# A gap of 64 bytes in front of the arena: it begins at a multiple of 128 bytes of a partition

## The reference

```python
for l in range(DEPTH):
    h = rms_norm(x, attn_norm[l])
    proj = h @ w_in[l]
    ...
    merged = g[:, :, 0] * o_a + g[:, :, 1] * o_b + g[:, :, 2] * o_c
    x = x + merged @ w_out[l]
    h2 = rms_norm(x, mlp_norm[l])
    x = x + jnp.square(jax.nn.relu(h2 @ w_up[l])) @ w_down[l]
```

## Time and profile before

| | |
|---|---|
| median of 3 runs | 2616.77 us (2615.76 to 2617.32) |
| profiled execution | 2626.14 us |
| span in it, first to last instruction | 2624.4 us |
| mean granted TensorE clock, share of full speed | 0.963 |
| TensorE busy with matmuls | 2446.8 us, 93% of the span |
| VectorE busy | 1946.6 us, 74% |
| ScalarE busy | 1388.1 us, 53% |
| read from main memory | 458.85 MB, 175 GB/s over the span |

### The profile page before, as it was taken

How to read it: one execution, slowest core, us unless ns; L and a number is a source line. 1 busy time by engine, 2 the same in 40 slices (tenths; PEclk the granted TensorE clock), 3 DMA queues, 4 the chain that set the end, 5 groups by cost and what they waited for, 6 DMA issues and landing times. The chain is left out here.

```text
span 2624.4 us, 46404 instructions
## 1 busy us (share of the span) xinstructions
PE 2446.8 (93%) x18912; PEld 2318.6 (88%) x18912; DVE 1946.6 (74%) x3284; ACT 1388.1 (53%) x2545; POOL 12.9 (0%) x20
## 2 busy tenths in 40 slices
PE   7899999988999999889998979999988999998998
PEld 6699999977999999879998879997788999976998
DVE  5477788754877886788887778886458889856884
ACT  6444555355455543646644556746463674434663
POOL 0000000000000000000000000000000000000000
PEclk8799999988999999989999999999989999988999
DMA  5124567721155678304565624573334457632552
GB/s 219 48 97 147 213 244 288 303 107 65 65 193 193 228 290 304 125 35 147 191 257 224 241 89 159 195 298 113 144 129 147 159 194 289 258 114 77 193 181 93
DMA packets 64084, 462.89 MB, mean 176 GB/s; under 512 B 7232, under 2 KB 7424, under 8 KB 8064
## 3 DMA queue, kind: packets, MB, share of 16 engines
q1 hardware_dynamic: 63872, 459.92, 47.5%
HBM read 458.85 MB, written 1.05 MB: 175 GB/s over the span
## 5 line engine op out<-in xcount | busy, mean ns | idle before, releaser
L770 PE MATMUL psum<-arena_rounded,upper_rounded 128*128 128x256 f32 (+2 forms) x5112 | 1450.9, 284 | 94.7 <-PEq L659 27.9
L771 PE MATMUL psum<-arena_rounded,upper_rounded 128*128 128x256 f32 (+2 forms) x5112 | 1437.4, 281 | 0.0
L772 PE MATMUL psum<-arena_rounded,ring_rounded 128*128 128x256 f32 (+2 forms) x5112 | 1436.8, 281 | 0.0
L770 PEld LDWEIGHTS psum<-arena_rounded,upper_rounded 128*128 128x128 f32 (+2 forms) x5112 | 972.1, 190 | 114.5 <-issue 62.7
L569 DVE TENSOR_TENSOR ring_rounded<-ring,upper_rounded 128x1024 fp32r<-128x1024 f32 (+4 forms) x958 | 840.0, 897 | 311.0 <-ACT upper_rounded L560 306.1
L560 ACT ACTIVATE upper_rounded<-ring 128x1024 fp32r<-128x1024 f32 (+4 forms) x958 | 751.6, 795 | 567.9 <-PE psum L772 483.5
L771 PEld LDWEIGHTS psum<-arena_rounded,upper_rounded 128*128 128x128 f32 (+2 forms) x5112 | 973.8, 190 | 0.7 <-issue 0.5
L772 PEld LDWEIGHTS psum<-arena_rounded,ring_rounded 128*128 128x128 f32 (+2 forms) x5112 | 972.3, 190 | 0.1
L591 DVE SCALAR_TENSOR_TENSOR ada_sum<-ring,small,ada_sum 128x1024 f32<-128x1024 f32 x168 | 214.9, 1279 | 1.3
L2369 DVE SCALAR_TENSOR_TENSOR arena<-psum,cols,arena 128x255 f32<-128x255 f32 (+1 forms) x352 | 153.3, 478 | 64.6 <-ACT arena L2336 61.5
L2336 ACT ACTIVATE arena<-psum,cols 128x256 f32<-128x256 f32 x176 | 89.5, 561 | 76.1 <-PE psum L772 76.0
(11 more groups left out here) (499 smaller groups left out, 2453.3 us busy)
## 6 DMA issues: line engine op xcount, KB each, us to landing
ring<-stream_dram SPq DMA_DIRECT2D x434, 1024.0 KB, 4.9
const<-const_dram SPq DMA_DIRECT2D x1, 1540.0 KB, 14.2
x<-x_dram SPq DMA_DIRECT2D x1, 1024.0 KB, 4.9
out_dram<-x SPq DMA_DIRECT2D x4, 256.0 KB, 2.1
cols<-cols_dram SPq DMA_DIRECT2D x1, 978.0 KB, 11.0
const<-const_dram SPq DMA_DIRECT2D x1, 67.0 KB, 4.6
pos<-positions_dram SPq DMA_DIRECT2D x1, 64.0 KB, 5.4
cols<-cols_dram SPq DMA_DIRECT2D x1, 4.0 KB, 4.4
```

What stands on the lines that cost most here:

```text
L770: pe.matmul(out, upper, x[0][:, b.k, :], start=(b.k == 0), stop=False)
L771: pe.matmul(out, upper, x[1][:, b.k, :], start=False, stop=False)
L772: ins = pe.matmul(out, lower, x[0][:, b.k, :], start=False, stop=(b.k == nk - 1))
```

## The change

`Chip.__init__` gets a small function that allocates a tensor that nobody uses, as large as is needed to bring the next start to `rest` modulo `edge`. It is called once, ahead of the arena, with 128: the arena and its rounded views move from byte 112,448 to 112,512. All other tensors stay where they are, and the instructions are the same.

```diff
         self.rounded_tensors = {}
 
+        def begin_at_multiple_of(edge, rest=0):
+
+            gap = (rest - (nc.sbuf_base + 31) // 32 * 32) % edge // 4
+            if gap:
+                sb(f"gap_{nc.sbuf_base}", gap)
+
         def sb_rounded_too(name, n, cuts=()):
 
             t = sb(name, n)
...
         self.small = sb("small", 176)
         self.stat = sb("stat", 8 * T)
         self.cos, self.pos = sb("cos", T), sb("pos", T, I32)
+        begin_at_multiple_of(128)
         self.arena = sb_rounded_too("arena", ARENA, ARENA_CUTS)
```

## The result

The changed kernel takes 2666.76 us (median of 4 runs, 2665.74 to 2667.93) against 2616.32 us of the kernel before on the same chip: a ratio of 1.0193, 95% interval 1.0175 to 1.0210. It is 50 us slower, and above the range that was forecast. The profiled execution took 2665.7 us.

What follows compares the result with a forecast made beforehand. The prediction took the spacing of TensorE's back-to-back float32r matmuls in project to bound the kernel. All terms summed to 0 against the median of 2616.8 us, giving 2617 us, range 2578 to 2640 us.

Steps and rivals of the forecast that it cites:

- What bounds the kernel: TensorE in project's three matmul lines: time is a count times a spacing, with 6.6 or 11.2 ns excess per matmul.
- One third at 113.3 ns and two thirds at 117.9 ns: Mix of spacings of L771's matmuls before the change, put at 116.3 ns on average.
- the long kind: Stretches before the change with 312 matmuls of L771 in 110 us, 117.9 ns apart; the short kind has 113.3 ns.
- The terms put at 0: Added instructions, waits, semaphores and transfers, VectorE and ScalarE work, and plain fp32 matmuls: each forecast to change nothing.
- the mix stays: Float32r matmuls keep their present shares of both spacings, 0 us; 2612 to 2622 us, chance 0.40.
- the address as such does not decide between the kinds: Float32r matmuls: both spacings occur at the same address modulo 128, so the choice looks settled when TensorE starts again.
- The upper bound: Float32r matmuls: if all took the long spacing, 5,000 x 4.5 ns = 23 us more.
- a spacing longer than any of today: Float32r matmuls: outside the range, unpriced; a still longer spacing shares the chance 0.27 with the long kind spreading.
- The slower one: Rival: the long spacing spreads at restarts as both streams start alike; 2640 us complete, 2628 half; chance 0.27.
- The faster one: Rival: the short spacing spreads at restarts, worth up to 45 us; 2572 us complete, some 2594 half; chance 0.29.
- The third: Rival: float32r matmuls lose their whole excess, 144 us, to 2473 us; chance 0.04.
- The cacheline rule: Lines are of 16 bytes, crossing costs below two hits per line; 64 and 128 are multiples, so sum 0.

Runs made afterwards that it cites:

- distance 192: The kernel before: moved columns begin 192 bytes beyond the held weights, both starts taken modulo 256 bytes; 2616.32 us.
- the trains: Unbroken rows of float32r matmuls behind short waits, in small kernels computing nothing of the reference, operand starts varied; spacings 113.3 to 123.4 ns with 128 held, 256 moved columns.
- distance 0: The changed kernel: moved columns and held weights begin alike modulo 256 bytes; 2666.76 us, ratio 1.0193 to the kernel before.
- the pair (192, 64): Against the kernel before, upper and arena moved: moved columns begin 192 bytes beyond upper's weights, 64 beyond the ring's, modulo 256; 2587.68 us, ratio 0.9884.
- its mirror image: Against the kernel before, upper and arena moved: moved columns begin 64 bytes beyond upper's weights, 192 beyond the ring's, modulo 256; 2634.37 us, ratio 1.0060.
- the one with both at 64 over: Full kernel with ring, upper and arena all beginning 64 bytes over a multiple of 128; 2667.01 us, ratio 1.0167 to the kernel before.
- The one at distance 128: Full kernel with a gap of 192 bytes ahead of the arena, moved columns 128 bytes beyond the weights modulo 256; 2653.39 us, ratio 1.0118.

## Why the prediction was wrong

**What bounds the kernel** was right. The spacing of the float32r matmuls is what the time is made of, it was named as the only place where the change could be worth anything large, and the loss lies there: 3.7 ns on each of 15,000. (One third at 113.3 ns and two thirds at 117.9 ns make 116.4 ns, not 116.3; the single starts give 117.8 ns for the long kind and so 116.3 ns. Nothing hangs on it.)

**The terms put at 0** held: instructions, transfers, VectorE and ScalarE are as before, by the groups after.

**The step that failed** is the last one, "I take the nearer value: the mix stays, 0 us". It rested on two things. One was that all stretches of before have the same address modulo 128 and still two spacings, "so the address as such does not decide between the kinds". That is right as far as it goes: at distance 192 the restart chooses, as the trains show (14 short, 7 long). But it says nothing about another distance, which has other kinds, and distance 0 has 120.0 ns alone. The other was L2671 to L2673, whose moved columns begin at a multiple of 128. As the prediction said itself, the relation of the two operands modulo 128 bytes is in these rows the same as everywhere before; they could not stand for the new one, and they did not: those very lines went from 233.3 to 226.4 ns.

**The upper bound** failed as well. "If all took the long one, 5,000 x 4.5 ns = 23 us more" bounds the unknown spacing by the spacings of today. Measured were 55 us by the same sum, since the new spacing is longer than both. A bound for an operation that the trace doesn't show was taken from the two values that it does, and the row which had a third value (116.7 ns per 256 columns) ought to have been a warning that there are more. The prediction did name a spacing longer than any of today, and left it outside its range without a price.

**The rivals.** The slower one named the right mechanism in outline: the two streams standing to each other in another way. It ended at 2640 us where the result is 2667 us, and it was off in form: not a lock into the long kind, but a new kind. The faster one, the short kind spreading, is what the pair (192, 64) does, at 2588 us; of its price of up to 45 us, 31 us were seen between the medians of one chip. The 45 us were counted in the profiled execution of before, but taken off the median, which lies 9.4 us lower. Between the profiled executions it is 42.8 us (2583.36 against 2626.14 us, on different chips and with clocks of 0.966 and 0.963). The third, the excess going altogether, was seen nowhere: no train of 256 moved columns and 128 held ones had less than 113.3 ns.

**Two rules that the runs do not bear out.** The cacheline rule of the Trainium skill's "SBUF — State Buffer" gives no difference between starts at multiples of 16 bytes; at the distances 32 and 64, both multiples of 16, the trains have 116.7 and 117.8 ns, and at 0 they have 120.0, so it does not describe this. By it the sum had been 0 as well. The same page of the Trainium skill, in the part "Who interferes with whom", says that TensorE's moving operand and its weight load have independent read ports and that TensorE never waits on anyone. The runs differ from that: the moved columns' spacing depends on where the loaded weights begin and on how many columns the load has (113.3 ns with 64 held columns, 120.0 ns with 128, at distance 0).

**What stays open.** The runs show the dependence, its period and its kinds, and not the mechanism in the chip; that both streams meet in something divided by address bits below 256 would fit and was only argued. At distances 0 and 192 the excess over the columns' own time comes in like portions, 6.7 and 13.3 ns with 256 moved columns, 13.3 and 20.0 ns with 512 (by the single starts), once, twice and three times 6.7 ns; 117.8 and 118.7 ns do not fit into that. It is also open what in a restart picks between two kinds, and why (192, 64) has one kind and its mirror image two; the few alike trains of other pairs leave open how many kinds those have.

## What to carry to other kernels

Where a kernel is a stream of float32r matmuls of 256 columns, compare the distance between starts with columns over 2.4 GHz (here 106.7 ns), and look for more than one steady value. If there is an excess, sweep the distance between the moved operand and the weights modulo 256 bytes in a small kernel of its own, for the pair of tensors that the real kernel uses, with many restarts of each; then place the tensors. Aligning one tensor for its own sake decides nothing by itself, and here the rounder start was the slower one.

## What the runs showed of the hardware that was not expected

At the full clock the steady spacing of float32r matmuls (128 held, 256 moved columns) depends on the distance of the two operands modulo 256 bytes: 113.3 ns at best (192 and 64, each only at times), 120.0 ns at 0 and 96, 123.4 ns at 4 bytes. For 512 moved columns the order is the other way: 226.6 ns at 0, 233.2 ns at 192.

Some placements have two steady spacings, held through 100 us and more and chosen anew at a restart. The kernel before was measured at 2615.8 to 2617.3 us on the first chip and at 2611.1 to 2634.2 us over 19 runs on the second; different choices at restarts would explain such a spread, and the changed kernel and the one with both at 64 over, which have a single kind, stayed within 2.2 and 0.9 us in 4 runs each. This was not traced run by run, and it can't be all: the kernel with the pair (192, 64), which has a single kind too, spread over 6.9 us in 4 runs. The one at distance 128 spread over 7.5 us, but its trace has two kinds (118.7 and 120.0 ns).
